# The experts' w_down chunks move from SyncE's DMA queue to ScalarE's in a decoder step with a mixture of experts

## The chip, the cores and the metric

The kernel runs on one core of a Trainium2 chip. The metric is the device time of one execution in microseconds (us); lower is better. All times below are of the kernel before the change.

## The reference, cut to what matters

One inference step of a decoder layer for 256 prompt tokens and 8 x 4 sample tokens, 288 rows of 1024 in float32. A state-space branch and an attention branch (with a paged cache of 2048 positions for the samples) are merged; after that comes a mixture of experts, where this case plays. Each token goes to 4 of 32 experts:

```python
def expert_block(args):
    xb, e = args
    gu = xb @ w_gu[e] + b_gu[e]
    g_lin = jnp.minimum(gu[:, 0::2], SWIGLU_LIMIT)
    up = jnp.clip(gu[:, 1::2], -SWIGLU_LIMIT, SWIGLU_LIMIT)
    act = (up + 1.0) * (g_lin * jax.nn.sigmoid(SWIGLU_ALPHA * g_lin))
    return act @ w_down[e] + b_down[e]
```

w_gu[e] is 1024 x 2048 (8 MB) and w_down[e] 1024 x 1024 (4 MB), so the 32 experts read 384 MB of weights.

## The kernel before, in words

Each engine has its own program; they meet on semaphores. All weights pass through a ring in SBUF of 12 slots of 1 MB (`ring`, 128 partitions x 2048 float32). One expert is 12 chunks: 8 of w_gate_up (128 rows each, one row of 8 KB a partition) and 4 of w_down (two rows of 4 KB a partition).

The chunks are numbered in the order in which TensorE uses them: gate-up of expert j (8 chunks), then w_down of expert j-1 (4 chunks), then gate-up of j+1. `gate_up_chunk` and `down_chunk` (L146, L151) give the number n, `chunk_slot` the slot. `c_free` counts the chunks that TensorE has used; the chunk n may be loaded when `c_free` is at least n - 11, which is when the chunk 12 before it in the same slot has been used. As the period is 12, eight slots always hold gate-up chunks and four always w_down chunks.

SyncE (SP) issues all these loads from one list (L484 to L503), in just this order, each behind its wait on `c_free`. The first 12 (gate-up of expert 0 and half of expert 1) are issued ahead of the loop, while the router runs. Behind the list it issues the 12 chunks of each extra job (L505 to L517): a job is an expert of which more than 64 rows are needed. With these inputs there is one extra job.

TensorE (L1315 to L1328) does for expert j: the bias matmul, 8 gate-up chunks (8 matmuls of 512 columns each), with the transposes of the activation of expert j-1 (`turn`) behind chunk 1 and a quarter of the selection of rows for the next four experts (`select`) behind chunk 3; then the four w_down chunks of expert j-1. `chunk` (L1300) waits until the chunk has landed.

ScalarE (L797 to L806) does for expert j, in order: `copy_act(j-1)` (the turned activation out of PSUM), `copy_x` (selected rows out of PSUM), `sigmoid(j)`, which waits for VectorE's clamped gate, and `copy_rows(j-1)` (L789), which waits until all four w_down chunks of expert j-1 have been used and copies the result out of PSUM. It issues no loads in the loop. GpSimd then writes these rows to DRAM (L853, 2 x 128 KB), from where they are gathered at the end, weighted and summed.

In the profile matmuls stand at L896 (`mm`) and transposes at L899 (`tr`).

Of the kernel before, what the change touches and what calls it, by code (L numbers as in the profile page):

```python
# [48 lines left out]
NE = 32  # L49
# [11 lines left out]
NSLOT = 12  # L61
# [84 lines left out]
def gate_up_chunk(j, k):  # L146

    return k if j == 0 else 12 * j - 4 + k


def down_chunk(j, c):  # L151

    return (12 * (j + 1) - 4 + 8 if j + 1 < NE else 12 * NE - 4) + c


def chunk_slot(n):
    return (n + FIRST) % NSLOT
# [12 lines left out]
def free_at(name, i=0):  # L170

    return USE0[name] + i
# [19 lines left out]
def build(nc, A):  # L192
    with ExitStack() as ctx:
        def sb(name, shape, dt=F32):
            return ctx.enter_context(nc.sbuf_tensor(name, shape, dt))

        def sem(name):
            return ctx.enter_context(nc.semaphore(name))
# [6 lines left out]
        ring = sb("ring", [P, NSLOT, 2048])  # L205
# [154 lines left out]
        loaded = [sem(f"loaded{s}") for s in range(NSLOT)]  # L360
# [40 lines left out]
        c_free, s_zero = sem("chunk_used"), sem("rows_zeroed")  # L401
# [3 lines left out]
        def slot(name):  # L405
            return ring[:, SLOT[name], :]
# [6 lines left out]
        wgu = A["w_gate_up"][0].rearrange("e (k p) n -> e k p n", p=P)  # L413
        wdn = A["w_down"][0].rearrange("e (c k p) n -> e c p k n", p=P, k=2)
# [3 lines left out]
        def extra_jobs(eng):  # L418

            eng.wait_ge(s_route, 1)  # L420
            return eng.value_load(jobi[0:1, 2 * NOVER:2 * NOVER + 1], min_val=0, max_val=NOVER)
# [4 lines left out]
        def pages_of(eng, kind, cache, b, slots=range(4)):  # L426

            for s in slots:
                name = f"{kind}{s}"
                eng.wait_ge(freed[SLOT[name]], free_at(name, b))  # L430
                for j in range(4):
                    page = eng.value_load(pages[0:1, ds(b * NPG + (4 * s + j), 1)], min_val=0, max_val=159)
                    eng.dma_start(ring[:, SLOT[name], j * 512:(j + 1) * 512],
                                  cache[ds(page, 1), :, :].rearrange("o p n -> p (o n)")).then_inc(
                                      s_vpool[s] if eng is nc.gpsimd else loaded[SLOT[name]], 16)
# [9 lines left out]
        @block.sync  # L445
        def _(sp):
            def load(name, src, dst=None):
                if free_at(name):
                    sp.wait_ge(freed[SLOT[name]], free_at(name))
                sp.dma_start(slot(name) if dst is None else dst, src).then_inc(loaded[SLOT[name]], 16)  # L450

            for t, (t0, n) in enumerate(TILES):
                sp.dma_start(x[0:n, t, :], xin[t]).then_inc(s_x, 16)
            sp.dma_start(pages[:, :], A["page_table"].rearrange("a b -> (a b)").unsqueeze(0)).then_inc(s_pages, 16)
            for k in range(8):
                load(f"w_in{k}", A["w_in"][0, k * P:(k + 1) * P, :])
            for k in range(8):
                load(f"w_gate{k}", A["w_gate"][0, k * P:(k + 1) * P, :])
            sp.wait_ge(s_pages, 16)

            pages_of(sp, "K", ck, 0)
            load("w_glu", A["ssm_w_glu"][0].rearrange("(k p) n -> p k n", p=P),
                 slot("w_glu").rearrange("p (k n) -> p k n", k=4))
            load("w_bs0", A["w_branch_ssm"][0, 0:256, :].rearrange("(k p) n -> p k n", p=P),
                 slot("w_bs0").rearrange("p (k n) -> p k n", k=2))
            sp.wait_ge(s_s5, 1)
            with sp.Fori(0, NB - 1) as b:

                pages_of(sp, "K", ck, b + 1, (0, 1, 2))
                pages_of(sp, "V", cv, b, V_BY_SP)  # L470
                pages_of(sp, "K", ck, b + 1, (3,))
            pages_of(sp, "V", cv, NB - 1, V_BY_SP)
            sp.wait_ge(s_eT, NB)
            load("w_bs1", A["w_branch_ssm"][0, 256:512, :].rearrange("(k p) n -> p k n", p=P),
                 slot("w_bs1").rearrange("p (k n) -> p k n", k=2))
            load("w_ba0", A["w_branch_attn"][0, 0:256, :].rearrange("(k p) n -> p k n", p=P),
                 slot("w_ba0").rearrange("p (k n) -> p k n", k=2))
            load("w_ba1", A["w_branch_attn"][0, 256:512, :].rearrange("(k p) n -> p k n", p=P),
                 slot("w_ba1").rearrange("p (k n) -> p k n", k=2))
            for i in range(4):  # L480
                load(f"w_out{i}", A["w_out"][0, i * 256:(i + 1) * 256, :].rearrange("(k p) n -> p k n", p=P),
                     slot(f"w_out{i}").rearrange("p (k n) -> p k n", k=2))

            def load_chunk(n, e, k):  # L484

                s = chunk_slot(n)
                if n < NSLOT:
                    sp.wait_ge(freed[s], _uses[s])
                else:
                    sp.wait_ge(c_free, n - NSLOT + 1)  # L490
                if k < 8:
                    sp.dma_start(ring[:, s, :], wgu[e, k, :, :]).then_inc(loaded[s], 16)
                else:
                    sp.dma_start(ring[:, s, :].rearrange("p (k n) -> p k n", k=2), wdn[e, k - 8, :, :, :]).then_inc(loaded[s], 16)

            for j in range(NE):
                for k in range(8):
                    load_chunk(gate_up_chunk(j, k), j, k)
                if j:
                    for c in range(4):  # L500
                        load_chunk(down_chunk(j - 1, c), j - 1, 8 + c)
            for c in range(4):
                load_chunk(down_chunk(NE - 1, c), NE - 1, 8 + c)  # L503
            extra = extra_jobs(sp)
            with sp.Fori(0, NOVER) as o:  # L505
                with sp.If(extra > o):
                    e = sp.value_load(jobi[0:1, ds(o, 1)], min_val=0, max_val=NE - 1)
                    for c in range(12):
                        s = chunk_slot(c)
                        sp.wait_ge(c_free, o * 12 + (NMAIN - NSLOT + c + 1))  # L510
                        if c < 8:
                            sp.dma_start(ring[:, s, :], wgu[ds(e, 1), c, :, :].rearrange("o p n -> p (o n)")).then_inc(loaded[s], 16)
                        else:
                            sp.dma_start(ring[:, s, :].rearrange("p (k n) -> p k n", k=2),
                                         wdn[ds(e, 1), c - 8, :, :, :].rearrange("o p k n -> p (o k) n")).then_inc(loaded[s], 16)
                with sp.Else():
                    sp.wait_ge(s_route, 1)  # L517
# [3 lines left out]
        def _(act):  # L521
# [249 lines left out]
            def copy_x(j, g, part):  # L771


                at_p = 4 * g + part
                act.wait_ge(e_part, at_p + 1)
                if g >= 2:
                    act.wait_ge(c_free, gate_up_chunk(4 * (g - 1) - 1, 7) + 1)
                nc.scalar.activation(xT[:, g % 2, 2 * part:2 * part + 2, :],  # L778
                                     psum[:, 4 + at_p % 2, :].rearrange("p (k c) -> p k c", k=2), ACT.Copy).then_inc(e_x, 1)

            def sigmoid(j):
                act.wait_ge(e_g, j + 1)
                nc.scalar.activation(sig, gg, ACT.Sigmoid, scale=ALPHA).then_inc(e_sig, 1)  # L783

            def copy_act(j):
                act.wait_ge(e_turn, j + 1)
                nc.scalar.activation(aT, psum[:, 3, :].rearrange("p (c q) -> p c q", c=4), ACT.Copy).then_inc(e_aT, 1)

            def copy_rows(j, used, written):  # L789
                act.wait_ge(c_free, used)  # L790
                if not (isinstance(written, int) and written == 0):
                    act.wait_ge(e_out, written)
                nc.scalar.activation(yS, psum[:, 2, :], ACT.Copy).then_inc(e_y, 1)  # L793

            for part in range(4):
                copy_x(0, 0, part)
            for j in range(NE):  # L797
                if j:
                    copy_act(j - 1)
                if j < NE - 4:  # L800
                    copy_x(j, j // 4 + 1, j % 4)
                sigmoid(j)
                if j:
                    copy_rows(j - 1, down_chunk(j - 1, 3) + 1, 32 * (j - 1))
            copy_act(NE - 1)
            copy_rows(NE - 1, NMAIN, 32 * (NE - 1))  # L806
            extra = extra_jobs(act)
            with act.Fori(0, NOVER) as o:
                with act.If(extra > o):
                    j = act.snap(o + NE)  # L810
# [1120 lines left out]
```

## Time and profile before

| | |
|---|---|
| time, median of 3 runs | 1794.6 us (1793.24 to 1797.31) |
| the profiled execution | 1794.52 us |
| its span | 1792.5 us |
| TensorE (PE) busy | 1519.5 us, 85% of the span |
| VectorE (DVE) busy | 593.9 us, 33% |
| ScalarE (ACT) busy | 371.9 us, 21% |
| GpSimd (POOL) busy | 83.7 us, 5% |
| moved by DMA | 536.17 MB, mean 299 GB/s |
| queue of SP (q1) | 493.00 MB |
| queue of ScalarE (q10) | 7.41 MB |
| w_gate_up, issued by SP | 264 DMAs of 1024 KB, median 20.9 us from issue to landing |
| w_down, issued by SP | 132 DMAs of 1024 KB, median 25.9 us from issue to landing |

The span goes from the first to the last instruction; the 2.0 us between it and the time of the same execution lie around it. A chunk of 1024 KB is 1.049 MB. The page cuts the span into 40 slices of 44.8 us; busy shares are in tenths. PEclk is TensorE's granted clock in tenths of its full 2.4 GHz. DMA is the mean busy share of the core's 16 DMA engines. "SPq" and "ACTq" are the queues of instructions with which these engines issue DMAs; the duration of such a row is that of the issue, not of the transfer.

### The profile page before, as it was taken

What the parts mean: (1) busy time and instruction counts of PE and PEld (TensorE: products, weight loads), DVE (VectorE), ACT (ScalarE), POOL (GpSimd) and SP (SyncE); (2) the same over time, 40 slices, a digit from 0 to 9 for tenths busy, and PEclk for the clock granted to TensorE, in tenths of its full rate; (3) what the DMA queues carried; (4) which work ended last, traced back from release to release, by engine and by line L of the source; (5) the groups of instructions that cost most, each with busy time, mean ns of one, the idle gap of its engine ahead of it and who ended that gap; (6) DMA issues with size and microseconds to landing.
All of it is one profiled execution on the core that took longest, in us unless ns stands there. A gap on an engine that the chain in (4) does not pass through costs nothing.

```text
span 1792.5 us, 19395 instructions
## 1 busy us (share of the span) xinstructions
PE 1519.5 (85%) x6579; PEld 718.0 (40%) x6579; DVE 593.9 (33%) x1166; ACT 371.9 (21%) x705; POOL 83.7 (5%) x151
## 2 busy tenths in 40 slices
PE   5977755888888897999999999999999999988880
PEld 4455534666665645333333323232332323222230
DVE  1487776888878316010101010101010110101004
ACT  1123224677776101000000000000000000000001
POOL 0000000001100000000000000000000000000002
PEclk9988876989988895899999999999999999999975
DMA  9410060787876423599999999999999999999944
GB/s 380 94 80 1 0 229 9 245 253 232 257 250 211 168 118 115 221 412 417 419 416 418 418 417 418 417 419 416 420 416 419 417 418 418 418 417 417 417 200 138
DMA packets 128690, 536.17 MB, mean 299 GB/s; under 512 B 20657, under 2 KB 21394, under 8 KB 92786
## 3 DMA queue, kind: packets, MB, share of 16 engines
q1 hardware_dynamic: 106914, 493.00, 69.5%
q0 software_dynamic: 10800, 34.87, 6.0%
q10 hardware_dynamic: 10912, 7.41, 1.3%
q8 instruction: 43, 0.70, 0.2%
q14 instruction: 21, 0.17, 0.0%
HBM read 519.36 MB, written 15.88 MB: 299 GB/s over the span
## 4 chain that ended last, share of the span: by engine, by line
PE 46%; DMA 33%; DVE 14%; issue 4%; ACT 2%; SPq 0%; DVEq 0%; POOLq 0%; POOL 0%; ACTq 0%
PE psum L896 41%; DMA ring<-in_w_gate_up 31%; PE psum L899 5%; DMA ring<-in_w_in 1%; DMA ring<-in_w_down 1%; DVE keys_low L1643 1%; DVE values_low L1647 1%; DVE ring L1654 1%; DVE ring L1529 1%; DVE arena L1897 1%; DVE ring L1530 1%; DMA ring<-expert_rows,rowi 0%; DVE arena L1509 0%; DVE ring L1507 0%; DVE ring L1524 0%
## 5 line engine op out<-in xcount | busy, mean ns | idle before, releaser
L896 PE MATMUL psum<-ring,arena 128*64 128x512 f32 (+3 forms) x3472 | 840.4, 601 | 76.1 <-DMA ring<-in_w_down 31.8
L896 PEld LDWEIGHTS psum<-ring,arena 128*64 128x64 f32 (+2 forms) x3472 | 256.7, 141 | 615.0 <-issue 433.7
L896 PE MATMUL psum<-arena 128*128 128x256 f32 (+8 forms) x798 | 286.4, 492 | 40.8 <-ACT ring L604 29.9
L1848 DVE TENSOR_SCALAR arena<-psum 128x256 f32<-128x256 f32 x66 | 24.9, 419 | 702.6 <-PE psum L896 702.6
L896 PEld LDWEIGHTS psum<-arena 128*128 128x128 f32 (+3 forms) x798 | 144.6, 217 | 186.8 <-issue 133.1
L896 PE MATMUL psum<-arena,ring 128*128 128x288 f32 x480 | 125.0, 424 | 7.4 <-DVE arena L1397 3.5
L899 PE MATMUL psum<-cst,ring 128*128 128x128 f32 (+1 forms) x640 | 93.5, 297 | 35.4 <-DVE keys_low L1643 21.7
L896 PEld LDWEIGHTS psum<-arena,ring 128*128 128x128 f32 x480 | 95.6, 200 | 35.7 <-DVE arena L1397 3.6
L899 PEld LDWEIGHTS psum<-cst,ring 128*128 128x128 f32 (+1 forms) x640 | 77.9, 158 | 50.3 <-DVE keys_low L1643 28.3
L899 PE MATMUL psum<-cst,arena 128*128 128x128 f32 (+3 forms) x319 | 54.2, 301 | 41.3 <-DVE arena L1383 14.1
L1643 DVE TENSOR_TENSOR keys_low<-psum,keys_high 128x512 fp32r<-128x512 f32 x128 | 82.1, 679 | 20.2 <-ACT keys_high L665 19.6
L853 POOL DMA_DIRECT2D expert_rows<-arena x66 | 34.2, 523 | 1157.4 <-ACT arena L793 1109.0
L1647 DVE TENSOR_TENSOR values_low<-ring,values_high 128x512 fp32r<-128x512 f32 x128 | 81.2, 680 | 9.4 <-ACT values_high L692 9.2
L783 ACT ACTIVATE arena<-arena 128x512 f32<-128x512 f32 x33 | 20.8, 631 | 280.8 <-DVE arena L1848 280.8
L692 ACT ACTIVATE values_high<-ring 128x512 fp32r<-128x512 f32 x128 | 72.4, 619 | 20.5 <-PE psum L896 20.1
L793 ACT ACTIVATE arena<-psum 128x512 f32<-128x512 f32 x33 | 19.7, 597 | 269.8 <-PE psum L896 269.8
L896 PE MATMUL psum<-keys_high,queries_split 128*64 128x256 f32 x256 | 74.4, 319 | 1.2 <-DVE keys_low L1643 1.2
L665 ACT ACTIVATE keys_high<-psum 128x512 fp32r<-128x512 f32 x128 | 70.8, 592 | 17.2 <-PE psum L899 15.7
L1842 DVE TENSOR_SCALAR arena<-cst 64x128 f32<-64x128 f32 x33 | 9.2, 277 | 188.0 <-PE psum L896 187.8
L899 PEld LDWEIGHTS psum<-cst,arena 128*128 128x128 f32 (+3 forms) x319 | 37.8, 157 | 77.2 <-issue 50.4
L896 PE MATMUL psum<-keys_low,queries_split 128*64 128x256 f32 x256 | 68.7, 297 | 0.0
L778 ACT ACTIVATE arena<-psum 128x512 f32<-128x512 f32 x32 | 19.1, 597 | 235.1 <-PE psum L896 235.1
(244 smaller groups left out, 903.4 us busy)
## 6 DMA issues: line engine op xcount, KB each, us to landing
ring<-in_w_gate_up SPq DMA_DIRECT2D x264, 1024.0 KB, 20.9
ring<-in_w_down SPq DMA_DIRECT2D x132, 1024.0 KB, 25.9
ring<-in_cache_k SPq DMA_DIRECT2D x128, 256.0 KB, 3.0
ring<-in_cache_v POOLq DMA_DIRECT2D x64, 256.0 KB, 4.2
ring<-in_cache_v SPq DMA_DIRECT2D x64, 256.0 KB, 3.0
expert_rows<-arena POOLq DMA_DIRECT2D x66, 128.0 KB, 6.0
ring<-in_w_in SPq DMA_DIRECT2D x8, 1024.0 KB, 16.3
ring<-in_w_gate SPq DMA_DIRECT2D x8, 1024.0 KB, 18.0
```

Source lines behind the costliest of these rows:

```text
L665: nc.scalar.activation(keyh[:, g % 2, :, (pg % 2) * P:(pg % 2 + 1) * P], psum[:, pg % 2, :].rearrange("p (h c) -> p h c", h=H), ACT.Copy). ...
L692: nc.scalar.activation(valh[:, pg % 3, :], ring[:, SLOT[f"V{pg // 4}"], (pg % 4) * 512:(pg % 4 + 1) * 512], ACT.Copy).then_inc(p_valh, 1)
L778: nc.scalar.activation(xT[:, g % 2, 2 * part:2 * part + 2, :], psum[:, 4 + at_p % 2, :].rearrange("p (k c) -> p k c", k=2), ACT.Copy).then ...
L783: nc.scalar.activation(sig, gg, ACT.Sigmoid, scale=ALPHA).then_inc(e_sig, 1)
L793: nc.scalar.activation(yS, psum[:, 2, :], ACT.Copy).then_inc(e_y, 1)
L853: pool.dma_start(ydram[ds(j * CAP, CAP), half * 512:half * 512 + 512], yS[half * CAP:half * CAP + CAP, :]).then_inc(e_out, 16)
L896: return nc.tensor.matmul(out, lhsT=a, rhs=b, start=start, stop=stop, skip_group_check=True)
L899: return nc.tensor.transpose(out, in_, ident[0:n, 0:n])
L1529: nc.vector.tensor_tensor_scan(flat(zr), flat(dec), flat(t1), 0.0, ALU.mult, ALU.add)
L1643: TT(keyl[place], psum[:, pg % 2, :].rearrange("p (h c) -> p h c", h=H), keyh[place], ALU.subtract).then_inc(p_keyl, 1)
L1647: TT(vall[:, pg % 3, :], ring[:, SLOT[f"V{pg // 4}"], (pg % 4) * 512:(pg % 4 + 1) * 512], valh[:, pg % 3, :], ALU.subtract).then_inc(p_val ...
L1848: ins = TS(gg[:, b * 256:b * 256 + 256], gu[:, b, 0::2], LIMIT, None, ALU.min)
```

## The change

The four loads of w_down of each expert leave SP's list. ScalarE issues them instead, by `load_down(j)`, each with the same wait on `c_free` and the same semaphore for the landing. For experts 0 to 30 it stands at the end of ScalarE's turn j, behind `copy_rows(j-1)`; for expert 31 it stands ahead of `sigmoid(31)`. The extra job's loads, w_down too, stay on SP.

```diff
--- before.py
+++ after.py
@@ -488,19 +488,11 @@
                     sp.wait_ge(freed[s], _uses[s])
                 else:
                     sp.wait_ge(c_free, n - NSLOT + 1)
-                if k < 8:
-                    sp.dma_start(ring[:, s, :], wgu[e, k, :, :]).then_inc(loaded[s], 16)
-                else:
-                    sp.dma_start(ring[:, s, :].rearrange("p (k n) -> p k n", k=2), wdn[e, k - 8, :, :, :]).then_inc(loaded[s], 16)
+                sp.dma_start(ring[:, s, :], wgu[e, k, :, :]).then_inc(loaded[s], 16)
 
             for j in range(NE):
                 for k in range(8):
                     load_chunk(gate_up_chunk(j, k), j, k)
-                if j:
-                    for c in range(4):
-                        load_chunk(down_chunk(j - 1, c), j - 1, 8 + c)
-            for c in range(4):
-                load_chunk(down_chunk(NE - 1, c), NE - 1, 8 + c)
             extra = extra_jobs(sp)
@@ -792,6 +784,15 @@
                     act.wait_ge(e_out, written)
                 nc.scalar.activation(yS, psum[:, 2, :], ACT.Copy).then_inc(e_y, 1)
 
+            def load_down(j):
+
+
+                for c in range(4):
+                    n = down_chunk(j, c)
+                    act.wait_ge(c_free, n - NSLOT + 1)
+                    act.dma_start(ring[:, chunk_slot(n), :].rearrange("p (k n) -> p k n", k=2), wdn[j, c, :, :, :]
+                                  ).then_inc(loaded[chunk_slot(n)], 16)
+
             for part in range(4):
                 copy_x(0, 0, part)
             for j in range(NE):
@@ -799,9 +800,13 @@
                     copy_act(j - 1)
                 if j < NE - 4:
                     copy_x(j, j // 4 + 1, j % 4)
+                if j == NE - 1:
+                    load_down(j)
                 sigmoid(j)
                 if j:
                     copy_rows(j - 1, down_chunk(j - 1, 3) + 1, 32 * (j - 1))
+                if j < NE - 1:
+                    load_down(j)
             copy_act(NE - 1)
```

## Rows read from the trace of the kernel before

**Rows 1.** The page: GB/s moved by DMA in its slices of 44.8 us.

```profile
GB/s 380 94 80 1 0 229 9 245 253 232 257 250 211 168 118 115 221 412 417 419 416 418 418 417 418 417 419 416 420 416 419 417 418 418 418 417 417 417 200 138
```

**Rows 2.** The critical chain, 841 to 1697 us: start, duration, what.

```profile
841.72 27.54 PE psum L896 x114
869.85 27.54 PE psum L896 x114
...
934.83 21.33 DMA ring<-in_w_gate_up
...
1678.57 19.05 DMA ring<-in_w_down
```

**Rows 3.** Windows: length, engines' busy us (instructions), clock, DMA share, GB/s.

```profile
734.00:746.60 12.60, 12.60 (x56) 4.83 (x54) 0.00 (x0) 1.88 (x2) 0.00 (x0) 1.00 0.89 341
...
746.60:752.60 6.00, 4.39 (x20) 1.39 (x14) 2.79 (x7) 0.63 (x1) 0.00 (x0) 1.00 0.94 293
752.60:780.00 27.40, 27.40 (x118) 9.61 (x117) 3.27 (x9) 2.39 (x4) 0.00 (x0) 1.00 1.01 407
...
1000.00:1500.00 500.00, 467.40 (x1913) 153.29 (x1912) 55.30 (x128) 39.39 (x65) 16.59 (x32) 1.00 1.02 418
```

**Rows 4.** SP's issues: full stretch 1100 to 1600, from 744.5, lone one at 734.

```profile
L494 SPq DMA_DIRECT2D ring<-in_w_down x67: 1242/4581/9462, 1097.6 to 1597.8; - x67
...
DMA to landing us min/median/max: 18.1/23.8/29.2
...
L494 SPq DMA_DIRECT2D ring<-in_w_down x4: 368/374/379, 744.5 to 749.7; - x4
...
DMA to landing us min/median/max: 4.8/4.8/4.8
```

**Rows 5.** Timeline at an expert's end: start, duration, engine, line, [idle before].

```profile
1040.53 0.60 ACT L793 ACTIVATE arena<-psum 128x512 f32<-128x512 f32 x1 [8.37 <-PE psum L896]
...
1042.32 3.65 PE L896 MATMUL psum<-ring,arena 128*64 128x512 f32 x16
...
1045.90 0.66 PE L899 MATMUL psum<-cst,arena 128*128 128x128 f32 x4
...
1046.60 0.60 ACT L787 ACTIVATE arena<-psum 128x512 f32<-128x512 f32 x1 [5.47 <-PE psum L899]
```

**Rows 6.** Timeline, ScalarE's first sigmoid.

```profile
750.45 0.63 ACT L783 ACTIVATE arena<-arena 128x512 f32<-128x512 f32 x1 [5.92 <-DVE arena L1848]
```

**Rows 7.** The start: issues of consts and x (two prompt halves, samples), landings, windows.

```profile
1.05 0.42 ACTq L530 DMA_DIRECT2D cst<-in_consts  x1
...
cst<-in_consts ACTq DMA_DIRECT2D x1, 964.0 KB, 6.6
...
L453 SPq DMA_DIRECT2D arena<-in_x_prompt x2: 402/411/420, 1.0 to 1.5; - x2
...
DMA to landing us min/median/max: 6.1/7.4/8.2
...
4.00:6.00 2.00, 0.00 (x0) 0.00 (x0) 0.00 (x0) 0.82 (x1) 0.00 (x0) 1.00 1.04 435
...
7.00:9.00 2.00, 0.00 (x0) 0.00 (x0) 0.00 (x0) 0.00 (x0) 0.00 (x0) 1.00 1.07 349
```

**Rows 8.** Timeline, SP's issues of the extra job's gate-up.

```profile
1682.70 10.84 SPq L512 DMA_DIRECT2D ring<-in_w_gate_up  x8
```

**Rows 9.** The tail: windows with the clock, a gap on PE, ring matmuls' min/median/max.

```profile
1703.00:1705.00 2.00, 2.00 (x10) 1.75 (x9) 0.00 (x0) 0.00 (x0) 0.00 (x0) 0.62 1.02 424
...
1735.06 1.11 PE L899 MATMUL psum<-cst,arena 128*128 128x128 f32 x4 [3.13 <-DVE arena L1859]
...
1735.00:1736.00 1.00, 0.94 (x4) 0.71 (x4) 0.01 (x1) 0.00 (x0) 0.00 (x0) 0.50 0.00 0
...
1741.00:1742.00 1.00, 1.00 (x6) 0.28 (x4) 0.00 (x0) 0.00 (x0) 0.00 (x0) 0.99 0.00 0
...
L896 PE MATMUL psum<-ring,arena x3072: 592/592/1113, 730.3 to 1699.0; 128*64 128x512 f32 x192
```

## The prediction

> **What bounds the kernel now.** I read the page's slices first. From slice 18 on the 16 DMA engines move 412 to 420 GB/s without a break, until the last two slices [rows 1]. That stretch is the expert loop. Then I read the list of the critical chain, which splits it in two. Up to some 930 us it is PE alone, one expert in 28.1 us; from 934.8 us each expert's chain ends in a wait for w_gate_up, and the last one for w_down, until 1697.6 [rows 2]; behind that comes PE's work for the one extra expert. The windows say that DMA is full in both parts, 418 GB/s later and 407 in 752.6 to 780 [rows 3]. So PE only lives on the 12 chunks that were loaded ahead, and the end of the loop is set by bytes: a chunk of 1.049 MB takes 2.51 us at 418 GB/s, and an expert (12 chunks and two row writes of 128 KB) 12.85 MB / 418 = 30.7 us. PE needs 28.1, so it has 2.6 us an expert to spare. Whatever leaves the DMA engines idle, or puts bytes ahead of the last w_down chunk, moves the end by as much.
>
> **What the change removes.** 128 waits and issues leave SP. In the full stretch SP spends a median 4.58 us on each w_down issue (0.37 us while its queue is short) [rows 4]. This looks like a bottleneck and isn't: the DMA share stays 1.02 [rows 3], and chunks land 18 to 29 us after issue [rows 4], so seven to eleven wait in the queue. I cost the freed SP time at nothing. The Trainium skill (Perfetto Trace Analysis, What "DMA-bound" means, and DMA Optimizations) says that an issuing engine whose track is solid with DMA slices can be the bottleneck, and that spreading issues over engines may then help. By that rule the change gains; the DMA share in the rows speaks against it. It is taken up as rival 4.
>
> **What it adds to ScalarE.** Four issues of 0.37 us, 1.5 us an expert. Their c_free waits are already met, because the row copy ahead of them waited for the whole of the previous w_down. Queued behind them are the copy of the turned activation, the copy of x and the sigmoid. ScalarE idles 5.47 us before that first copy [rows 5], so 1.5 us is hidden, with 4 us left. For the last expert the four issues wait for w_gate_up chunks 0 to 3 ahead of the sigmoid, which isn't due until chunk 7: nothing.
>
> **What it moves, 1: the first w_down.** Now its chunks are issued from 744.5 on, as gate-up chunks 4 to 7 of expert 0 are used. Then they stand behind sigmoid(0), which starts at 750.45 and takes 0.63 [rows 6]: issue at 751.1. A lone chunk takes 4.8 us to land [rows 4], 2.51 of that transfer, so 2.3 is latency; I put 1.5 of it ahead of the bytes, which gives 752.6. From 734 to 746.6 the window holds 12.6 us x 341 GB/s = 4.3 MB, just the four chunks of w_gate_up that SP issued (4.2). So in 746.6 to 752.6 nothing would be moved, where now 6.0 x 293 = 1.76 MB are [rows 3], together with the 0.1 before 1.86 MB. At 418 GB/s that is **+4.5 us**, and a stage that stays full never gives it back. Bounds: 3 us (latency ahead of the bytes nil) to 6.
>
> **What it moves, 2: order in steady state.** With one queue bytes come in the order in which PE uses them. Now w_down(j) stands in a second queue from the moment of its issue, beside w_gate_up. How do two queues share the engines? The start shows it: consts (ACT, 964 KB, rows of 7.7 KB) and x_prompt (SP, 2 x 512 KB, rows of 4 KB) are issued together. Consts land at 1.05 + 6.6 = 7.65, the first half of x at 7.1, but the second at 8.9 [rows 7]. In the 1.25 us from 7.65 to 8.9, at 349 GB/s [rows 7], 0.44 MB of x were still to come; so of its 1.05 MB SP had moved some 0.61 while ACT moved 0.99, 1.6 to 1. That is nearer to one row of each in turn (1.9 to 1) than to equal bytes. Here w_gate_up has rows of 8 KB and w_down of 4: **2 to 1**. While both queues hold work a w_down chunk takes 7.5 us and a w_gate_up chunk 3.8.
>
> Does this make the loop late? Take E, the end of w_down(j-1) on PE (1040.4 in the rows, 0.1 ahead of the row copy). The row copy ends 0.7 later, ACT issues at E + 0.8. SP's next chunk can be issued only when the first gate-up chunk is used; two take 3.65 on PE, so one is done at 1042.32 + 1.9 = E + 3.9 [rows 5]. So w_down is alone for 3.1 us (1.23 chunks); the other 2.77 take 20.9, the row writes 0.6, landing 2.3, the last chunk on PE 1.9. The next E is 0.8 + 3.1 + 20.9 + 0.6 + 2.3 + 1.9 = 29.6 us later, under the 30.7 of the bytes. Each us of w_gate_up backlog at the issue adds 3, so it settles at 0.35 us of backlog, DMA still full, PE's 2.6 us of stall in one piece before the last w_down chunk instead of in many. **Cost 0**, but with a margin of only 1.1 us in 30. In this state all of w_gate_up(j+1) has landed by E; in the kernel before about none of it has.
>
> **What it moves, 3: the tail.** The same interleaving holds for the last w_down against the extra expert's w_gate_up, which SP now issues in the list behind it [rows 8]. Count from E, the end of w_down(29). w_down(30) is alone, done at 0.8 + 0.35 + 0.6 + 10.05 = 11.8. w_down(31) is already queued. But SP gets its first extra chunk off when gate-up chunk 4 of the last expert is used, at 1.9 + 5 x 1.8 + 0.65 = 11.5, and the others in time. From 11.8 on eight extra chunks take 8 x 3.8 = 30.1 and four of w_down 4 x 7.5 = 30.1: all eight come ahead of the last w_down chunk. In the kernel before none does. PE can do nothing with them until w_down(31) is done, and they are hidden there today: **+20.1 us**. Bounds: 10 (equal bytes) to 20.
>
> **The clock behind it.** In that tail PE works 1.9 and waits 5.6 us, three times. In the extra expert a gap of 3.1 us (1732 to 1735) took the granted clock from 1.00 to 0.50 [rows 9], 1.2 instead of 2.4 GHz. So I expect 1.2 GHz on the last w_down chunk (+1.9; a matmul took 592 to 1113 ns [rows 9]) and on the first 2.9 us of the extra selection (from some 1700.6, 3 us behind the last wait), which had 2.4 until some 1703.5 [rows 9] (+2.9). From there on I take the clock as it was. **+4.8**, bounds 0 and 6.
>
> **Sum.** The profiled execution took 1794.5 (span 1792.5 and 2.0 around it), 0.1 from the median 1794.6. 1794.5 + 4.5 + 0 + 20.1 + 4.8 = **1824**, with 1815 to 1832 for this case.
>
> **Rivals.**
> 1. The queues share by equal bytes. For it: the start shows the ratio only to some 20%. Then four extra chunks come ahead, 10.0, and the clock costs 3: 1794.5 + 4.5 + 10 + 3 = 1812. The Trainium skill (DMA: Bandwidth & Descriptors, Queues, rings and completion order) has the engines change rows only after a whole packet of some 9 to 17 descriptors, which for 8 against 16 rows a chunk and engine comes near to this case; no run here shows it yet.
> 2. Bytes are served in the order of issue whatever the queue: only the late first w_down stays, 1799.
> 3. The loop from issue to landing to row copy becomes the bound in every expert. PE's stall in one piece of 2.6 us is near the 3.1 that lost the clock; with 1.2 GHz for 6.5 us, as from 1734.5 to 1741 [rows 9], PE needs 28.1 + 3.25 = 31.4, 0.6 over the bytes, for 28 experts +17: 1841. Or w_down starts 0.9 us later than I take it, three times that less the margin of 1.1: 1.6 an expert, +45: 1869. Against it: the margin is there on paper.
> 4. The other side, faster: two queues lift the rate. The tail and the fill cost 29.4 in 960 us, so it decides from 418 x 960 / 930.6 = 431 GB/s on. Of the windows at the start with two queues one has 435 and one 349 [rows 7], which is no clear sign of it. At 435: 1794.5 + 29 - 38 = 1786.
> 5. Nothing moves, because the extra chunks are late for another reason and the fill is caught up: 1795.
>
> **Chances.** Forecast 0.47, rival 1 0.14, rival 2 0.10, rival 3 0.19, rival 4 0.05, rival 5 0.05. Range 1800 to 1856: it takes in the forecast, rival 1, the nearer half of 2 and most of 3. A measurement here tells 0.2% (3.6 us) from no change. Faster 0.05; same 0.05 and the lower part of rival 2, 0.08; slower 0.87.
>
> **What would show it.** In the profile after: no bytes for some 5 us before 752; DMA share 1.0 and 30.7 us an expert on the chain after that, PE waiting once an expert for w_down rather than w_gate_up; w_down landings near 25 us with w_gate_up's under it; the last wait for w_down ending near 1722 with the extra w_gate_up landed before it; a clock of 0.5 there. Wrong if the expert's period is above 31.5 (rival 3), if the last w_down wait ends by 1705 (rival 2), or if the rate leaves 418.

## The result and the profile after

| | before | after |
|---|---|---|
| time, median | 1794.2 us (4 runs) | 1864.8 us (4 runs) |
| ratio | | 1.0391, 95% interval 1.0359 to 1.0423 |
| profiled execution | 1794.5 us | 1866.6 us |
| its span | 1792.5 us | 1864.6 us |
| PE busy | 1519.5 us | 1555.1 us |
| DMA, mean | 299 GB/s | 288 GB/s |
| queue of SP / of ScalarE | 493.00 / 7.41 MB | 358.78 / 141.64 MB |

The change makes the kernel 70.6 us slower. Slower was forecast, but 1824 us, with a range that ended at 1856. Of all kernels below only the one with rows of 2 KB scatters by more than 1.5% at an unchanged clock (1977.5 to 2025.2 us): its ratio goes by its two shorter executions, and its profile is of the longest.

In the page after, the slices of 46.6 us from slice 18 on should be set against [rows 1]. Where the kernel before has 412 to 420 GB/s in each, the numbers now go up and down between 370 and 420:

```profile
GB/s 374 111 47 1 0 225 68 250 240 253 237 198 311 112 111 76 366 399 387 420 380 382 408 370 405 377 416 389 408 376 389 419 376 420 381 390 419 381 96 132
```

The windows (length, busy us of PE, PEld, DVE, ACT and POOL with their instructions, clock, DMA share, GB/s) put numbers on it. They answer to [rows 3]; the loop after the fill is the fourth, and the last row is the loop of the kernel before:

```profile
734.00:746.60 12.60, 12.60 (x54) 4.88 (x52) 0.00 (x0) 1.88 (x2) 0.00 (x0) 0.95 0.81 306
746.60:752.60 6.00, 4.39 (x21) 1.35 (x18) 1.63 (x5) 0.63 (x1) 0.00 (x0) 1.00 0.14 57
752.60:780.00 27.40, 27.40 (x118) 9.65 (x117) 4.16 (x9) 1.83 (x3) 0.00 (x0) 1.00 1.01 408
...
780.60:1727.90 947.30, 859.00 (x3387) 287.94 (x3387) 95.29 (x221) 68.45 (x113) 29.99 (x58) 0.94 0.97 395
```

```profile
779.50:1658.00 878.50, 825.17 (x3387) 270.61 (x3387) 95.23 (x221) 68.40 (x113) 30.09 (x58) 1.00 1.02 418
```

The two loop windows hold the same 29 experts, 3387 matmuls each: 947.3 us against 878.5. From them and from the tail the loss adds up in three terms.

- **The loop**: 947.3 x (1 - 395/418) = 52 us in which bytes were not moved. (The window is 68.8 us longer than that of the kernel before. In the other 17 us bytes were moved: the window has 374.2 MB against 366.9, since w_gate_up of the next expert has landed here by the time that an expert ends, and hadn't in the kernel before. That is order and no loss.)
- **The fill**: up to 752.6 us 12.6 x 306 + 6 x 57 GB/s = 4.20 MB against 12.6 x 341 + 6 x 293 = 6.05 [rows 3], 1.85 MB less, 4.4 us.
- **The tail**: SP's extra chunks are issued from 1739.8 on (SP's line in the timeline answers to [rows 8]), the first lands 9.5 us later, at 1749.3, and five have landed by 1767.4, when the last w_down chunk does; the sixth follows at 1768.2. Some 5.7 chunks came ahead, 14.3 us. (By bytes it is a little less: 405.5 MB from 734 us to the last landing against 400.4 before, 5.1 MB or 12.2 us. From 1727.9 to 1739.8 us the engines moved only 346 GB/s, another 2.0 us.)

Together 70.7 us. The end of the last wait for w_down moved by 69.8 us (1697.6 to 1767.4), the two profiled executions are 72.1 apart.

The critical chain (start, duration, what) shows how the loop loses. In [rows 2] the waits end on w_gate_up. Now they all end on w_down, and there is not one an expert: the chain has 16 in 29 experts, mostly in every second:

```profile
820.34 22.07 PE psum L901 x94
843.89 31.92 DMA ring<-in_w_down
...
885.25 22.07 PE psum L901 x94
908.80 32.11 DMA ring<-in_w_down
...
1020.46 27.54 PE psum L901 x114
1048.58 22.07 PE psum L901 x94
1071.62 1.52 ACTq L793
1073.18 32.09 DMA ring<-in_w_down
...
1737.97 29.42 DMA ring<-in_w_down
```

Take the pair of experts around 1070.7 us. The timeline gives the row copies, E in the terms of the prediction, at 1042.5, 1070.7, 1109.0 and 1141.4: 28.1, 38.4 and 32.4 us. In the first of them w_down, issued at once, lands in 5.1 to 22.2 us. In the second it takes up to 32.1. Issues and landings by ScalarE's instructions at 1042.6 and at 1070.7, then SP's of the same second expert:

```profile
L793 ACTq DMA_DIRECT2D ring<-in_w_down x4: 374/536/694, 1042.6 to 1044.1; - x4
...
DMA to landing us min/median/max: 5.1/12.2/22.2
...
L793 ACTq DMA_DIRECT2D ring<-in_w_down x4: 374/486/1520, 1070.7 to 1073.2; - x4
DMA to landing us min/median/max: 12.6/22.9/32.1
...
L491 SPq DMA_DIRECT2D ring<-in_w_gate_up x8: 327/328/328, 1074.4 to 1090.7; - x8
...
DMA to landing us min/median/max: 8.4/13.3/17.0
```

The windows of the three experts, and some ahead of, in and behind the wait for w_down:

```profile
1045.80:1070.70 24.90, 24.90 (x111) 8.71 (x108) 2.83 (x7) 1.85 (x4) 0.00 (x0) 1.00 1.02 419
1070.70:1109.00 38.30, 30.24 (x119) 9.89 (x119) 3.05 (x7) 2.40 (x4) 1.04 (x2) 0.93 0.93 383
1109.00:1141.40 32.40, 32.40 (x119) 10.93 (x120) 4.08 (x10) 2.42 (x4) 1.03 (x2) 0.87 0.97 395
1067.00:1069.00 2.00, 2.00 (x12) 0.71 (x10) 0.00 (x0) 0.00 (x0) 0.00 (x0) 1.00 1.01 422
1097.00:1105.00 8.00, 1.94 (x8) 0.48 (x8) 0.00 (x0) 0.00 (x0) 0.00 (x0) 0.93 1.03 425
1105.30:1109.00 3.70, 3.69 (x9) 0.84 (x9) 0.00 (x0) 0.00 (x0) 0.00 (x0) 0.50 0.11 44
1109.00:1112.00 3.00, 3.00 (x4) 1.08 (x4) 1.28 (x4) 0.60 (x1) 1.03 (x2) 0.50 0.55 169
```

While PE waits for w_down (1097 to 1105, 1.94 us busy of 8) the DMA engines run at 425 GB/s: they bring w_gate_up, which SP could queue, next to w_down, which PE needs. When w_down is there at last (1105.3), SP's queue has run empty, and the engines drop to 44 GB/s until the expert ends at 1109.0, and to 169 in the 3 us behind that. That is the idle time, and the granted clock is at 0.50, 1.2 GHz, after the wait.

### The profile page after: what moved, and what is told of

It reads as the page before. It is cut to its first block, busy times and chain, and to the rows that moved or that the text cites. A ratio compares the mean times of both kernels' runs of the same rounds, so it can differ in the third digit from the quotient of the medians.

```text
span 1864.6 us, 19395 instructions
## 1 busy us (share of the span) xinstructions
PE 1555.1 (83%) x6579; PEld 738.6 (40%) x6579; DVE 594.5 (32%) x1166; ACT 371.7 (20%) x705; POOL 83.9 (5%) x151
## 3 DMA queue, kind: packets, MB, share of 16 engines
q1 hardware_dynamic: 72098, 358.78, 48.7%
q10 hardware_dynamic: 45728, 141.64, 19.7%
## 4 chain that ended last, share of the span: by engine, by line
PE 50%; DMA 29%; DVE 13%; issue 4%; ACT 2%; ACTq 1%; SPq 0%; DVEq 0%; POOLq 0%; POOL 0%
PE psum L901 45%; DMA ring<-in_w_down 27%; PE psum L904 5%; DMA ring<-in_w_in 1%; ACTq L793 1%; DVE keys_low L1648 1%; DVE values_low L1652 1%; DVE ring L1659 1%; DVE ring L1534 1%; DVE arena L1902 1%; DVE ring L1535 1%; DMA ring<-expert_rows,rowi 0%; ACT arena L785 0%; DVE arena L1514 0%; DVE ring L1512 0%
## 5 line engine op out<-in xcount | busy, mean ns | idle before, releaser
L901 PE MATMUL psum<-ring,arena 128*64 128x512 f32 (+3 forms) x3472 | 861.0, 622 | 112.6 <-DMA ring<-in_w_down 95.0
L901 PEld LDWEIGHTS psum<-ring,arena 128*64 128x64 f32 (+2 forms) x3472 | 270.3, 145 | 652.2 <-issue 524.0
L901 PE MATMUL psum<-arena 128*128 128x256 f32 (+8 forms) x798 | 299.5, 510 | 40.5 <-ACT ring L596 29.6
L901 PEld LDWEIGHTS psum<-arena 128*128 128x128 f32 (+3 forms) x798 | 150.1, 225 | 200.2 <-issue 146.2
L904 PEld LDWEIGHTS psum<-cst,ring 128*128 128x128 f32 (+1 forms) x640 | 76.8, 157 | 50.3 <-DVE keys_low L1648 28.5
L785 ACT ACTIVATE arena<-psum 128x512 f32<-128x512 f32 x33 | 19.7, 597 | 353.6 <-PE psum L901 353.6
L684 ACT ACTIVATE values_high<-ring 128x512 fp32r<-128x512 f32 x128 | 72.5, 619 | 23.0 <-PE psum L901 22.6
L657 ACT ACTIVATE keys_high<-psum 128x512 fp32r<-128x512 f32 x128 | 70.7, 592 | 16.8 <-PE psum L904 15.9
L901 PE MATMUL psum<-values_high,exps_split 128*64 128x512 f32 x128 | 54.0, 422 | 15.7 <-DVE values_low L1652 14.0
```

The source lines that it names most:

```text
L657: nc.scalar.activation(keyh[:, g % 2, :, (pg % 2) * P:(pg % 2 + 1) * P], psum[:, pg % 2, :].rearrange("p (h c) -> p h c", h=H), ACT.Copy). ...
L684: nc.scalar.activation(valh[:, pg % 3, :], ring[:, SLOT[f"V{pg // 4}"], (pg % 4) * 512:(pg % 4 + 1) * 512], ACT.Copy).then_inc(p_valh, 1)
L901: return nc.tensor.matmul(out, lhsT=a, rhs=b, start=start, stop=stop, skip_group_check=True)
L904: return nc.tensor.transpose(out, in_, ident[0:n, 0:n])
```

## The experiments

**The theory (A).** The queues take rows in turn. With 8 KB rows in one and 4 KB in the other, w_down gets a third of the bytes, and its last chunk lands 32 us after issue whenever SP has work queued; that makes the expert late, SP's queue empties, the DMA engines idle, the next w_down finds them free, and so on. **Rivals:** the late issue behind the row copy is what costs, however the bytes are shared (B); a second hardware queue costs by itself (C).

### Rows of 8 KB for w_down

```diff
-        wdn = A["w_down"][0].rearrange("e (c k p) n -> e c p k n", p=P, k=2)
+        wdn = A["w_down"][0].rearrange("e (c p k) n -> e c p (k n)", p=P, k=2)
...
-                last = tr(psum[:, 3, c * P:(c + 1) * P], xa[:, c * P:(c + 1) * P])
+                last = tr(psum[:, 3, c * P:(c + 1) * P], xa[:, 256 * (c // 2) + c % 2:256 * (c // 2) + 256:2])
...
-                    act.dma_start(ring[:, chunk_slot(n), :].rearrange("p (k n) -> p k n", k=2), wdn[j, c, :, :, :]
+                    act.dma_start(ring[:, chunk_slot(n), :], wdn[j, c, :, :]
```

> The change, with w_down loaded in rows of 8 KB instead of 4 (a partition takes two neighbouring rows; the transposes of the activation are strided to match), so that both queues hold rows of the same size. Theory A (the queues take rows in turn, so w_down gets one third of the bytes, its last chunk lands 33 us after issue whenever SP has work queued, and the loop swings between a late expert and one with the DMA engines idle): with equal rows w_down gets half, a chunk takes 5.0 us instead of 7.3 beside w_gate_up, the last lands some 22 us after issue, ahead of its due time; the DMA engines stay full at 418 GB/s, experts at 30.7 us, PE waits for w_gate_up. Left are the first w_down (4.5 us) and some 5 extra chunks ahead in the tail (11 us): 1810 us. Theory B (the late issue behind the row copy is what costs, however the bytes are shared): unchanged, 1860 to 1870. Theory C (a second hardware queue costs by itself): unchanged.

Measured: 1803.3 us, 1.0045 of before (1.0031 to 1.0059). Four fifths and more of the loss is gone, with the same issue points and the same two queues; A had 1810, B and C 1860 and more. w_down's issues and landings of one expert, the chain, and the window of the loop:

```profile
L792 ACTq DMA_DIRECT2D ring<-in_w_down x4: 334/465/1420, 1046.0 to 1048.3; - x4
DMA to landing us min/median/max: 10.2/17.0/22.8
...
1037.93 29.90 DMA ring<-in_w_gate_up
...
1000.00:1500.00 500.00, 476.48 (x1943) 164.51 (x1943) 56.10 (x130) 39.98 (x66) 16.53 (x32) 0.98 1.01 422
```

The last w_down lands 22.8 us after issue, PE waits for w_gate_up again, and DMA is full. The swing is not gone, though: where A had experts at 30.7 us, they take 28.2 us and up to 35.9, and it costs nothing as the engines never idle. The rate is 422 GB/s, not 418, which had not been expected and is followed up below.

### Issue ahead of the row copy

```diff
-                if j:
-                    copy_rows(j - 1, down_chunk(j - 1, 3) + 1, 32 * (j - 1))
                 if j < NE - 1:
                     load_down(j)
+                if j:
+                    copy_rows(j - 1, down_chunk(j - 1, 3) + 1, 32 * (j - 1))
```

> The change with ScalarE's four issues put ahead of the row copy of the same turn instead of behind it, so that each chunk is issued when its slot comes free, up to 6 us earlier for the first. Theory A: w_down now has 9 us to itself before SP can issue, 3 to 4 chunks; it is never late and the loop is full again, 30.7 us an expert; left are the first w_down and the tail: 1808 to 1816 us. Theory B: better too, and nearly as good, since the lateness is gone. Theory C (the second queue by itself): stays at 1860.

Measured: 1822.1 us, 1.0145 (1.0117 to 1.0172). The rate in the loop is as foreseen, 418 GB/s. Two waits of the chain and the window:

```profile
1302.83 29.98 DMA ring<-in_w_down
...
1364.43 29.95 DMA ring<-in_w_down
...
1000.00:1500.00 500.00, 472.59 (x1909) 162.43 (x1906) 53.30 (x124) 38.76 (x64) 16.53 (x32) 0.97 1.02 418
```

But A also had w_down never late, and that is not so. PE waits for it 18 times between 780 and 1690 us, 51.4 us in all, and from 1275 to 1550 us the experts take 28 and 33.3 us in turn, with one wait in the chain every 61.6 us. Those two together are twice the 30.7 us of the bytes. So the swing by itself isn't what costs; what costs is a long expert that outlasts the transfers queued for it.

The total is above the 1808 to 1816 expected. There the tail had been taken at 10 to 18 us; here all eight extra chunks land ahead of the last w_down (20.1 us), and with the fill that is 1819. The same form without them settles it, below. C is out.

### Late issue in one queue

```diff
                 if j:
+                    if j == 1:
+                        sp.wait_ge(e_sig, 1)
+                    else:
+                        sp.wait_ge(e_y, j - 1)
                     for c in range(4):
                         load_chunk(down_chunk(j - 1, c), j - 1, 8 + c)
+            sp.wait_ge(e_aT, NE - 1)
```

> The kernel before, all loads on SP, but each expert's w_down is held until ScalarE's row copy (for expert 0 its sigmoid, for expert 31 its copy of the activation), the moment at which the changed kernel issues it. Theory A: in one queue the order stays, seven or more chunks are queued ahead, so lateness costs only the first w_down: 1794 + 4.5 = 1799 us. Theory B (lateness is the cause): 1840 to 1865. Theory C says 1799 as well.

Measured: 1798.6 us, 1.0028 (1.0017 to 1.0039), 4.6 us more than before, where the fill had 4.5. In one queue the lateness costs the loop nothing; B is out as a cause by itself.

### Only experts 1 to 28, only expert 0, only 29 to 31

`BY_ACT` is the range of experts whose w_down ScalarE issues; SP keeps the others in its list.

```diff
+BY_ACT = range(1, 29)     # middle_only; range(0, 1) in first_only, range(29, 32) in tail_only
...
+                if j and j - 1 not in BY_ACT:
+                    for c in range(4):
+                        load_chunk(down_chunk(j - 1, c), j - 1, 8 + c)
```

> The change for experts 1 to 28 only; w_down of experts 0 and 29 to 31 stays in SP's list. All theories: the loop's share of the loss, without the late first w_down and without extra chunks ahead of the last. By the byte count of the two profiles that share is 51 of 70 us: 1794 + 51 = 1845 us, with the swing of 28 and 37 us between experts; if the first w_down or the tail start the swing, much less, under 1810.

> Only w_down of expert 0 moves to ScalarE's queue (issued behind its sigmoid), all others stay in SP's list. Theory A: nothing is moved for 4.5 us while the ring refills, and the loop never gets it back: 1794 + 4.5 = 1798.5 us. If the fill is caught up while PE lives on the chunks loaded ahead: 1794.

> Only w_down of experts 29, 30 and 31 moves to ScalarE's queue. Theory A: extra chunks of w_gate_up come ahead of the last w_down, by the profile of the changed kernel 5.7 of them (14.3 us), at most 8 (20 us): 1808 to 1814 us. If the extra chunks are hidden wherever they come: 1794.

Measured: middle 1844.3 us, 1.0282 (1.0261 to 1.0302), +50.3; first 1798.0, 1.0019 (1.0009 to 1.0030), +3.6; tail 1814.9, 1.0118 (1.0101 to 1.0135), +20.5. The first two are as expected, the tail is 1 us above its upper end: all eight extra chunks land ahead of the last w_down, and in its chain the last wait for w_down ends at 1720.2, 22.6 us after that of the kernel before.

```profile
1655.58 24.16 DMA ring<-in_w_gate_up
1679.74 40.44 DMA ring<-in_w_down
1720.22 1.96 PE psum L911 x8
```

The parts add up to 74 us, the whole change costs 71: in it 5.7 extra chunks get ahead instead of eight, presumably because the swing leaves less work in SP's queue when the tail begins.

### Rows of 2 KB for w_down

```diff
+        wdn = A["w_down"][0].rearrange("e (c k p) (h n) -> e c p h k n", p=P, k=2, h=2)
...
+                mm(psum[0:CAP, 2, :], lhs, w[:, r * 512:r * 512 + 512], False, c == 3 and r == 1)
+                last = mm(psum[CAP:P, 2, :], lhs, w[:, D + r * 512:D + r * 512 + 512], False, c == 3 and r == 1)
```

> The change, with w_down in rows of 2 KB (four a partition, the two column halves apart; the matmuls read them there). Theory A: rows are taken in turn, 8 KB against 2, so w_down gets a fifth of the bytes while SP has work, 12.6 us a chunk. SP's 8 chunks then take 25.1 us, w_down gets 1.23 chunks ahead of them, 2 beside and 0.8 behind them: 0.8 + 3.1 + 25.1 + 1.9 + 0.6 + 2.3 + 1.9 = 35.7 us for every expert, no swing, since all of w_gate_up has landed by then: 29 x 5 = 145 us over the kernel before, plus 4.5 and 10 to 20 for fill and tail, 1955 to 1965 us. Theory B (lateness) or C (the second queue by itself): about 1865.

Measured: 1986.1 us, 1.1066 (1.1023 to 1.1109), from two executions of 1977.5 and 1994.7 us; the other two took 2008.8 and 2025.2. All four are more than the 1955 to 1965 of A, and far from the 1865 of B and C. In the profile, which is of the longest, most experts take 38 to 40 us and some 32; two of the waits in the chain, one expert's issues, and the loop:

```profile
829.80 33.62 DMA ring<-in_w_down
...
868.88 33.40 DMA ring<-in_w_down
...
L793 ACTq DMA_DIRECT2D ring<-in_w_down x4: 609/662/845, 827.8 to 829.8; - x4
DMA to landing us min/median/max: 6.0/16.9/33.6
...
1000.00:1500.00 500.00, 411.67 (x1598) 137.41 (x1596) 46.84 (x109) 32.72 (x54) 13.48 (x26) 0.90 0.87 346
```

The last chunk landed at 829.8 + 33.6 = 863.4, 35.6 us after E (827.8), where A had 33.8. The rest is the clock: it had taken 1.9 us for the last chunk on PE and this took 3.7, at 1.2 GHz after a wait of 8 us. The two sum to 39.3 an expert. A had no experts of 32 us.

The share of the queues can be read from the last two w_down chunks of one expert, which land behind each other while SP has w_gate_up queued: 4.9 us apart in rows8k (1066.2 and 1071.1), 7.4 in the changed kernel (1097.9 and 1105.3) and 11.8 here (851.6 and 863.4). Between them the engines moved 423, 425 and 341 GB/s; here they had stopped by the end, and the pair of chunks before, 12.0 us apart, had 409. So w_down got 0.51, 0.34 and 0.21 of the bytes, where one row of each queue in turn gives 1/2, 1/3 and 1/5.

### Issue later still

```diff
                 if j:
                     copy_act(j - 1)
+                    if j < NE - 1:
+                        load_down(j - 1)
...
-                if j < NE - 1:
-                    load_down(j)
```

(In turn 31 ScalarE issues w_down(30) and w_down(31) behind that copy.)

> The change with ScalarE's four issues one step later still, behind its next copy of the turned activation. Theory A: SP's next chunk is now issued first (E + 6.6 at 1.2 GHz) and w_down only at E + 10.3. SP's 8 chunks keep it at 3.8 us a chunk to E + 34.8, w_down has 3.3 chunks by then, the rest, the row writes and the landing end at E + 39.6, the last chunk and the bias on PE at 1.2 GHz take 3.7: 43.3 us for every expert, no swing: 29 x 12.6 = 365 us more, with fill and tail 2150 to 2190 us. A theory in which the lateness only shifts each issue by its own amount says 30.7 + 10 = 41 at most; one in which it is hidden, 1865.

Measured: 2146.2 us, 1.199 (1.194 to 1.204). Moving four issues by 6 us costs 281 us more, 9 us an expert, and the swing is gone, as A says. Two pieces of the chain:

```profile
1010.81 29.88 DMA ring<-in_w_down
1040.73 8.88 PE psum L902 x28
...
1051.70 29.49 DMA ring<-in_w_down
1081.24 9.11 PE psum L902 x28
...
1000.00:1500.00 500.00, 391.74 (x1444) 123.88 (x1444) 40.21 (x94) 29.66 (x49) 13.47 (x26) 0.88 0.79 309
```

An expert takes 41 us (1081.24 - 1040.73 = 40.5 in these rows) where 43.3 had been worked out: the issue comes 6.1 us behind E instead of 10.3, since the clock is back early enough. This run does not speak against the rival of a plain shift (41 at most). Its 29 experts take 1197.3 us against 947.3, 250 more; a shift of 6.1 us in each gives 177, and PE, with a clock of 0.86 instead of 0.94, is busy for 928 us instead of 859, so the two come to 246. What rules that rival out is rows8k, where the same issue points cost the loop nothing.

### The row size in one queue, and the two controls

```diff
-                    sp.dma_start(ring[:, s, :].rearrange("p (k n) -> p k n", k=2), wdn[e, k - 8, :, :, :]).then_inc(loaded[s], 16)
+                    sp.dma_start(ring[:, s, :], wdn[e, k - 8, :, :]).then_inc(loaded[s], 16)
```

before8k is the kernel before with this, and with the first two pairs of lines of the diff of rows8k; the extra job's w_down is loaded in the same way. middle8k is rows8k and middle_early is early, both with `BY_ACT = range(1, 29)`.

> The kernel before (one queue), with w_down in rows of 8 KB and the transposes strided to match. In the profile of rows8k the DMA engines moved 422 GB/s in the loop where the others have 418. If that comes from the longer rows and not from the two queues, it holds here too: 960 us x (1 - 418/422) = 9 us less, 1785 us, faster than both kernels. If it comes from having two queues: 1794.

> w_down in rows of 8 KB everywhere; ScalarE issues it for experts 1 to 28, SP for 0 and 29 to 31. Theory A: with equal rows the second queue costs the loop nothing, and fill and tail are as in before8k: 1786 us, against 1844 for the same split with rows of 4 KB (middle_only). If the loop still lost something beside fill and tail: 1790 to 1800.

> ScalarE issues w_down of experts 1 to 28 ahead of its row copy (as in early), SP those of 0 and 29 to 31; rows of 4 KB. Theory A: the DMA engines never go idle in the loop, so it ends as in the kernel before: 1794 us. If the early form still loses in the loop: over 1800.

Measured: before8k 1786.3 us, 0.9949 (0.9933 to 0.9966), **faster than both kernels**. The last wait for w_down ends at 1662.45 + 27.55 = 1690.0 instead of 1697.6:

```profile
1662.45 27.55 DMA ring<-in_w_down
1690.05 1.96 PE psum L895 x8
...
1000.00:1500.00 500.00, 472.52 (x1927) 158.06 (x1928) 55.63 (x130) 39.98 (x66) 17.58 (x34) 1.00 1.01 422
```

So 422 GB/s comes from the longer rows, not from a second queue. Against before8k, rows8k (1803.3) has lost 17 us, not 9: that is what the change costs with equal rows, and it lies in the fill and the tail, as the last wait for w_down ends 15 us later (1705.1). middle8k: 1788.9, 0.9964 (0.9951 to 0.9977), 2.6 us above before8k with intervals that overlap: with equal rows the second queue costs the loop nothing that these runs can tell. middle_early: 1794.2, 0.9999 (0.9988 to 1.0010): an issue some 6 us earlier costs nothing either, with rows of 4 KB. Both moved the loads of 28 experts to ScalarE, and neither gains by it.

## Why the prediction was wrong

**What bounds the kernel: right.** Bytes set the end of the loop. Every variant with a full DMA in the loop ends as the kernel before, but for fill, tail and the rate.

**The freed SP time and ScalarE's issues at nothing: right.** Middle_early and middle8k show it: w_down of 28 experts is off SP there, and neither is faster than the same rows in one queue. The issues took 0.37 to 1.5 us each and ran beside the row copy: both start at E (1109.0), where I had put the first issue 0.8 us behind. The rule that the prediction took from the Trainium skill (Perfetto Trace Analysis, What "DMA-bound" means), that a solid queue of issues can be the bottleneck, does not hold here; the profile's DMA share was the better guide.

**The fill: right.** 4.5 us forecast, 4.4 by bytes; 3.6 and 4.6 us as time in the two runs that have it alone.

**How the queues share: right.** 2 to 1 was forecast from the start of the trace; in the profile after, w_down's first chunk lands at 1070.7 + 12.6 = 1083.3 and its fourth at 1073.2 + 32.1 = 1105.3, 7.3 us a chunk (7.5 forecast). Equal bytes (rival 1) is out by rows8k and rows2k. The Trainium skill (DMA: Bandwidth & Descriptors, Queues, rings and completion order) lets an engine change its queue only after a whole packet of descriptors. If a packet were always one chunk's part on an engine (8 rows of 8 KB or 16 of 4 KB), the bytes would be shared equally, as rival 1 had it, and these runs disagree with that; if packets hold equal numbers of rows, the shares are the measured ones. The runs don't tell turns of one row from turns of several.

**"It settles at 0.35 us of backlog, DMA still full ... Cost 0": this is the step that failed.** The working ahead of it was right: an expert with no backlog takes 29.6 us or PE's 28.1, and each us of backlog adds 3. I then looked for the backlog at which the expert takes the 30.7 us of its bytes and took the loop to stay there. It can't. An expert queues 30.7 us of transfers, and as many are served as it lasts: from a backlog r the next one is r + 30.7 - (29.6 + 3r) = 1.1 - 2r. A deviation from 0.35 comes back doubled, with the other sign, and grows until it meets the two stops, PE's 28.1 us and an empty queue. With w_down leaving at E instead of E + 0.8 the 29.6 becomes 27.2 (3.9 us alone, 1.55 chunks; 2.45 x 7.53 + 0.6 + 2.3 + 1.9 behind), and behind a long wait PE needs 3.7 instead of 1.9 at 1.2 GHz. So r = 0 gives 28.1 (PE is the bound), then r = 2.6, then 27.2 + 7.8 + 1.8 = 36.8, in which the transfers are done 3.5 us early and the engines idle; then r = 0 again. That is 1.75 us an expert, 51 us over 29 of them. The profile has 28.1 and 36 to 38 in turn, now and then with a third between, and 52 us. The loss is the 3.5 us of idle engines, not the turning itself: a long expert of 33.3 us (30.7 + 2.6) would cost nothing, and early has just that. The margin of 1.1 us was none: the one point of rest is not stable.

**Rival 3 had the place and nearly the number** (the loop from issue to landing as the bound, 1841 to 1869), but with another reason, a fixed excess in every expert. With its chance of 0.19 I cut the range at 1856. A mechanism with a gain of three, whose sign hung on 1 us of an estimated latency, should have had more.

**The tail: right in kind, large by 6 us.** 20.1 us forecast; 14.3 in the profile after, 20.5 where it was alone. **The clock behind it: not shown.** 4.8 us forecast; from the last wait to the end there are 97.2 us after (1864.6 - 1767.4) and 94.9 before (1792.5 - 1697.6), so 2.3. But this stretch takes 91.8 us in tail_only and 96.3 in before8k, so 2.3 is no more than it varies by.

**Open:** whether a turn is one row of each queue or several, and what the clock costs in the loop. The mean clock is 0.94 instead of 1.00 there, and the expert behind a long wait takes up to 32.4 us instead of 28.1; but that one also lets SP's queue fill less, which makes the one after it shorter. No run takes the one from the other.

## What to carry to other kernels

One queue keeps an order; two don't. Work that is due later but queued beside work due now takes its share, and the share goes by the size of the rows, so the stream with short rows waits longest. Where loads are issued by what they release, ask not only whether the loop fits in its time, but what a delay of 1 us makes of the next turn: a factor above one means a swing, and the swing costs as soon as a late turn lasts longer than the work that is queued for it. A queue whose issues are slow while the DMA engines are full is waiting for them, and freeing the engine that issues them won nothing here.

## What the runs showed of the hardware

- Two hardware queues, SP's with rows of 8 KB: a chunk of 1.049 MB in the other took 4.9 us with rows of 8 KB, 7.3 with 4 KB and 11.8 to 12.0 with 2 KB; 2.51 alone at 418 GB/s. In the experts shown the last of the four chunks landed 22.8, 32.1 and 33.6 us after its issue.
- Rows of 8 KB instead of 4 in a third of the bytes raised the full DMA rate from 418 to 422 GB/s, 8 us here.
- A DMA that stands behind an ACTIVATE in ScalarE's program is issued together with it, not behind it (1109.05 and 1109.04 us); nothing in the program makes it wait for the copy's end:

```profile
1109.04 0.60 ACT L785 ACTIVATE arena<-psum 128x512 f32<-128x512 f32 x1 [16.89 <-PE psum L901]
...
1109.05 2.15 ACTq L793 DMA_DIRECT2D ring<-in_w_down  x4
```
